# Square sums of q and k as two f32r products a tile later, in a stick-breaking attention trunk

## What is computed

```python
def odd_mixer(h, w_qkv, q_norm_g, k_norm_g, w_out):
    q, k, v = jnp.split(h @ w_qkv, 3, axis=-1)
    q = rms_norm(q.reshape(bsz, s_len, SB_HEADS, SB_HEAD_DIM), q_norm_g)   # 8 heads of 128
    k = rms_norm(k.reshape(bsz, s_len, SB_HEADS, SB_HEAD_DIM), k_norm_g)
    ...
# stick_breaking, for each block of queries:
    z = jnp.einsum('bhqd,bhkd->bhqk', qb, kb).astype(jnp.float32) * scale
    log_keep = jnp.where(mask, jax.nn.log_sigmoid(-z), 0.0)
    acc = lax.cumsum(log_keep, axis=3, reverse=True) - log_keep
    w = jnp.where(mask, jnp.exp(jax.nn.log_sigmoid(z) + acc), 0.0)
    outs.append(jnp.einsum('bhqk,bhkd->bhqd', w.astype(vb.dtype), vb))
```

## Time and profile before

| what | value |
|---|---|
| median of 3 runs | 2447.64 us (2446.96 to 2449.67) |
| the profiled execution | 2449.88 us, its span 2448.1 us |
| TensorE busy | 2408.2 us, 98% of the span |
| VectorE, ScalarE, GpSimd busy | 1583.0, 830.4, 595.5 us |
| mean granted clock of TensorE | 0.996 |
| TensorE's waits for others in 1180 to 1700 us | 6.6 us in all, 1.9 us the largest group |

### The profile page before, as it was taken

One profiled execution on the slowest core, in us unless ns is written; L12 is line 12 of the kernel. 1 busy time (PEld: TensorE's weight loads), 2 busy tenths in 40 slices (PEclk: granted clock), 3 DMA queues, 4 the chain that ended last, 5 costly groups with the idle time before them and its releaser, 6 DMA issues.

```text
span 2448.1 us, 31399 instructions
## 1 busy us (share of the span) xinstructions
PE 2408.2 (98%) x10938; PEld 1987.2 (81%) x10938; DVE 1583.0 (65%) x2543; ACT 830.4 (34%) x1489; POOL 595.5 (24%) x964
## 2 busy tenths in 40 slices
PE   6999999999999999999999999998999999999999
PEld 5888888888888888888778888887888888888887
DVE  6636777388667665765777777776587666665222
ACT  4102333144333340000466666664253333320001
POOL 4344333300000004455143333334100000015340
PEclk9999999999999999999999999999999999999999
DMA  8543446623342349666211111116323333456331
GB/s 284 173 138 99 134 133 205 204 78 112 104 129 95 112 129 351 225 228 210 78 53 44 44 43 44 43 54 222 121 74 108 121 104 111 129 202 229 147 121 69
DMA packets 268606, 324.40 MB, mean 133 GB/s; under 512 B 8458, under 2 KB 168356, under 8 KB 268324
## 3 DMA queue, kind: packets, MB, share of 16 engines
q1 hardware_dynamic: 239552, 257.45, 31.9%
q10 hardware_dynamic: 28900, 65.04, 7.5%
HBM read 240.67 MB, written 81.79 MB: 132 GB/s over the span
## 4 chain that ended last, share of the span: by engine, by line
PE 91%; DVE 3%; DMA 2%; issue 2%; POOL 1%; ACT 1%; SPq 0%; DVEq 0%; ACTq 0%; POOLq 0%
PE psG L911 24%; PE psG L917 23%; PE psG L916 23%; PE psZ L917 4%; PE psZ L916 4%; PE psZ L911 4%; PE psM L1347 1%; PE psO L911 1%; PE psG L1388 1%; PE psO L916 1%; PE psO L917 1%; PE psZ L1377 1%; DMA ada_raw<-in_ada_w 1%; DMA w_raw<-in_ev_w_in 1%; PE psM L962 1%
## 5 line engine op out<-in xcount | busy, mean ns | idle before, releaser
L883 POOL TENSOR_SCALAR w_split<-w_raw 128x256 fp32r<-128x256 f32 x448 | 199.4, 471 | 1773.3 <-DMA w_raw<-in_ffn_w_down 1091.6
L911 PE MATMUL psG<-h_hi,w_split 128*128 128x512 f32 x1080 | 436.1, 404 | 7.2 <-DVE h_lo L2168 3.8
L916 PE MATMUL psG<-h_lo,w_split 128*128 128x512 f32 x1080 | 425.4, 394 | 0.0
L917 PE MATMUL psG<-h_hi,w_split 128*128 128x512 f32 x1080 | 425.3, 394 | 0.0
L887 POOL TENSOR_TENSOR w_split<-w_raw,w_split 128x256 fp32r<-128x256 f32 x448 | 359.2, 832 | 0.0
L2714 DVE SCALAR_TENSOR_TENSOR xT<-psG,mod,xT 128x512 f32<-128x512 f32 x192 | 143.0, 749 | 212.3 <-PE psG L917 211.9
L911 PE MATMUL psG<-hid,w_split 128*128 128x512 f32 x704 | 276.3, 393 | 0.0
L911 PE MATMUL psG<-h_hi,f_w 128*128 128x512 f32 x704 | 275.2, 391 | 0.6 <-PE psG L917 0.6
L917 PE MATMUL psG<-hid,w_split 128*128 128x512 f32 x704 | 274.5, 390 | 0.0
L916 PE MATMUL psG<-hid,w_split 128*128 128x512 f32 x704 | 274.3, 390 | 0.0
L916 PE MATMUL psG<-h_lo,f_w 128*128 128x512 f32 x704 | 274.3, 390 | 0.0
(11 more groups left out here) (300 smaller groups left out, 4027.7 us busy)
## 6 DMA issues: line engine op xcount, KB each, us to landing
hid<-f_spill SPq DMA_DIRECT2D x44, 1024.0 KB, 9.4
f_spill<-f_stg SPq DMA_DIRECT2D x80, 512.0 KB, 2.7
f_raw<-in_ffn_w_gate SPq DMA_DIRECT2D x44, 512.0 KB, 3.9
f_raw<-in_ffn_w_up SPq DMA_DIRECT2D x44, 512.0 KB, 4.6
w_raw<-in_ffn_w_down SPq DMA_DIRECT2D x44, 512.0 KB, 6.1
ada_raw<-in_ada_w SPq DMA_DIRECT2D x40, 512.0 KB, 4.1
ada_raw<-in_ada_w ACTq DMA_DIRECT2D x40, 512.0 KB, 4.5
w_raw<-in_ev_w_in SPq DMA_DIRECT2D x28, 512.0 KB, 4.0
```

The costliest lines, as they stand in the source:

```text
L883: nc.gpsimd.tensor_scalar(slot[:, 0, part], raw[:, part], 1.0, 1.0, ALU.mult, ALU.mult).then_inc(hi_done, 1)
L911: mm = nc.tensor.matmul(o, st[0], mv[0], start=first, stop=False, **kw)
L916: nc.tensor.matmul(o, st[0], mv[1], start=False, stop=False, **kw)
L917: return nc.tensor.matmul(o, st[1], mv[0], start=False, stop=end, **kw)
```

## The change

Three edits. First, the square sums of q and k: ScalarE squares the copy twice, once to float32 and once to f32r (`s_sqh`), VectorE subtracts the two (`square_low`, behind the softplus of the slot) to `s_sql`, and TensorE makes two f32r products with the matrix of -1 in place of the float32 product; the factor -1/128 goes into ScalarE's Ln. The statistic and what follows it (`qkv_misc`, `qkv_second`, `qkv_dve`) go from slots 2, 4, 6, 8 to slots 3, 5, 7, 9 (`SUMMED`); v's steps stay. Copy and squares stay in slots 2, 4, 6, 8. Second, in `out1` GpSimd's slab 4 waits for the weights of all tiles but the last, and slab 5 for the last. Third, in `first_conv` slab 2's first four blocks go ahead of `first_direct`.

```diff
--- before.py
+++ after.py
@@ -110,6 +110,7 @@
 
 TAKEN = [2, 4, 6, 8, 10, NT]
 DONE = {t: e for e, t in enumerate(TAKEN)}
+SUMMED = {t + (e < 4): e for t, e in DONE.items()}
 ZRING = 3
 SRING = 3
 
@@ -280,7 +281,10 @@
         s_raw = [at("s_raw", WO + 32 * KB, [H]), at("s_raw1", WO + 8 * KB, [H])]
         s_sq = [at("s_sq", WO + 34 * KB, [H]), at("s_sq1", WO + 10 * KB, [H])]
         s_r = [at("s_r", WO + 36 * KB, [H]), at("s_r1", WO + 12 * KB, [H])]
-        s_t = at("s_t", WO + 38 * KB, [H])
+        s_t_off = (WO + 38 * KB, WO + 14 * KB)
+        s_t = [at(f"s_t{n}", s_t_off[n], [H]) for n in range(2)]
+        s_sqh = [at(f"s_sqh{n}", s_t_off[n], [H], F32R) for n in range(2)]
+        s_sql = [at(f"s_sql{n}", (WO + 34 * KB, WO + 10 * KB)[n], [H], F32R) for n in range(2)]
         s_vsb = at("s_vsb", WO + 40 * KB, [H])
         s_osb = at("s_osb", WO + 42 * KB, [2, H])
 
@@ -410,6 +414,8 @@
         fh_in = [sem(f"fh_in{n}") for n in range(4)]
         s_raw_cp = sem("s_raw_cp")
         s_rs = sem("s_rs")
+        s_sqh_in = sem("s_sqh_in")
+        s_sql_in = sem("s_sql_in")
         s_qk3 = sem("s_qk3")
         s_vhi = sem("s_vhi")
         s_zd = sem("s_zd")
@@ -871,6 +877,8 @@
                         if phase == "out1" and s == 4:
                             pool.wait_ge(s_qk3, 12 * SB_HEADS)
                         if phase == "out1" and s == 4:
+                            pool.wait_ge(s_wst, 3 + 2 * (NT * SB_HEADS - 1))
+                        if phase == "out1" and s == 5:
                             pool.wait_ge(s_wst, 3 + 2 * NT * SB_HEADS)
 
                         if phase == "out1" and s == 3:
@@ -1035,9 +1043,9 @@
                 x_turn(6)
                 k_major(0, (1,), (2, 3))
                 x_turn(7)
+                k_major(0, (2,), range(4))
                 pe.wait_ge(misc_read, M("norm0", 0, 1) - 1)
                 first_direct()
-                k_major(0, (2,), range(4))
                 first_cols(1, 0)
                 first_cols(1, 1)
                 x_root_pe(1)
@@ -1342,9 +1350,11 @@
                 hd = head[0] + i * head[1]
                 s, h, n = qkv_step(phase, e)
                 if s < 2:
-                    pe.wait_ge(s_raw_cp, 4 * hd + (n + 1))
-                    sq = s_sq[qk_pair(phase, n)]
-                    misc(phase, i, 2 * off + e, [lambda: nc.tensor.matmul(psM[:], ones_head, sq[:], start=True, stop=True)])
+                    pe.wait_ge(s_sql_in, 4 * hd + (n + 1))
+                    pair = qk_pair(phase, n)
+                    misc(phase, i, 2 * off + e, [
+                        lambda: nc.tensor.matmul(psM[:], split_c[:, 2], s_sqh[pair][:], start=True, stop=False),
+                        lambda: nc.tensor.matmul(psM[:], split_c[:, 2], s_sql[pair][:], start=False, stop=True)])
                 else:
                     bank_wait(pe, phase, i, 2 * off + e)
                     misc(phase, i, 2 * off + e, [lambda j=j: nc.tensor.transpose(psM[:, P * j:P * j + P], s_vsb[:, P * j:P * j + P], ident)
@@ -1426,8 +1436,8 @@
                         qkv_piece(phase, i, off, sum(PIECES[:t]) + n)
 
                 def stat(t):
-                    if t in DONE:
-                        qkv_misc(phase, i, off, DONE[t], hd_next)
+                    if t in SUMMED:
+                        qkv_misc(phase, i, off, SUMMED[t], hd_next)
 
                 for t in range(1, NT):
                     slot(hd, par, t, True, lambda: fill(t), lambda: stat(t))
@@ -1944,6 +1954,7 @@
                     fn(raw[:], psG[:, bank(phase, s)], ACT.Copy).then_inc(bank_read[bank(phase, s)], 1)
                     bank_wait(act, phase, i, s)
                     fn(sq[:], raw[:], ACT.Square).then_inc(s_raw_cp, 1)
+                    fn(s_sqh[pair][:], raw[:], ACT.Square).then_inc(s_sqh_in, 1)
                 else:
 
                     if phase != "qkv0":
@@ -1958,7 +1969,7 @@
                 m, h, n = qkv_step(phase, e)
                 if m < 2:
                     root = s_r[qk_pair(phase, n)]
-                    fn(root[:], psM[:], ACT.Ln, bias=EPS).then_inc(misc_read, 1)
+                    fn(root[:], psM[:], ACT.Ln, scale=-1.0 / HEAD, bias=EPS).then_inc(misc_read, 1)
                     act.wait_ge(misc_read, M(phase, i, 2 * off + e))
                     fn(root[:], root[:], ACT.Exp, scale=-0.5).then_inc(s_rs, 1)
                 else:
@@ -2021,8 +2032,8 @@
                         qkv_first(phase, i, off, DONE[t], hd_next)
 
                 def second_step(t):
-                    if t in DONE:
-                        qkv_second(phase, i, off, DONE[t], 1 - par, hd_next)
+                    if t in SUMMED:
+                        qkv_second(phase, i, off, SUMMED[t], 1 - par, hd_next)
 
                 for t in range(1, NT):
                     slot(hd, t, True, lambda: first_step(t), lambda: second_step(t))
@@ -2778,13 +2789,21 @@
                     dve.wait_ge(s_qk3, n0)
                     gain = qg[:, 0:1] if m == 0 else vecB[:, B_K:B_K + 1]
                     pair = qk_pair(phase, n)
-                    V.scalar_tensor_tensor(s_t[:], s_raw[pair][:], gain, s_r[pair][:], ALU.mult, ALU.mult).then_inc(s_qk3, 1)
+                    V.scalar_tensor_tensor(s_t[pair][:], s_raw[pair][:], gain, s_r[pair][:], ALU.mult, ALU.mult).then_inc(s_qk3, 1)
                     dve.wait_ge(s_qk3, n0 + 1)
-                    split([q[:, half(h)] for q in s_qk[par][m]], s_t[:], s_qk3, n0 + 2, s_qk3)
+                    split([q[:, half(h)] for q in s_qk[par][m]], s_t[pair][:], s_qk3, n0 + 2, s_qk3)
                 else:
                     dve.wait_ge(s_vhi, hd * 2 + (h + 1))
                     vv = slice(4 * h, 4 * h + 4)
                     V.tensor_tensor(s_v[par][1][:, vv], psM[:].rearrange("p (j c) -> p j c", c=P), s_v[par][0][:, vv].bitcast(F32), ALU.subtract).then_inc(misc_read, 1)
+
+            def square_low(phase, i, off, e, head):
+
+                hd = head[0] + i * head[1]
+                m, h, n = qkv_step(phase, e)
+                pair = qk_pair(phase, n)
+                dve.wait_ge(s_sqh_in, hd * 4 + (n + 1))
+                V.tensor_tensor(s_sql[pair][:], s_sq[pair][:], s_sqh[pair][:].bitcast(F32), ALU.subtract).then_inc(s_sql_in, 1)
 
             def softplus(hd, t):
 
@@ -2834,8 +2853,10 @@
             def head(phase, i, off, hd, hd_next, par):
 
                 def step(t):
-                    if t in DONE:
-                        qkv_dve(phase, i, off, DONE[t], 1 - par, hd_next)
+                    if t in SUMMED:
+                        qkv_dve(phase, i, off, SUMMED[t], 1 - par, hd_next)
+                    if t in DONE and DONE[t] < 4:
+                        square_low(phase, i, off, DONE[t], hd_next)
 
                 for t in range(1, NT):
                     slot(hd, t, True, lambda: step(t))
@@ -2845,12 +2866,20 @@
 
                 qkv_dve("qkv0", 0, 0, e, 0, (0, 0))
 
+            def first_low(e):
+
+                square_low("qkv0", 0, 0, e, (0, 0))
+
             for k in range(KT):
                 norm2.h_tile(1, k)
+                if k in (2, 3):
+                    first_low(k - 2)
                 if k == 5:
                     first_step(0)
             first_step(1)
             first_step(2)
+            first_low(3)
+            first_low(4)
             dve.wait_ge(x_out, 32)
             softplus(0, 0)
             first_step(3)
```

## The result

The changed kernel takes 2524.46 us (median, 2521.3 to 2527.11), against 2448.65 us for the kernel before: 1.0312 times as long, with a 95% interval of 1.03 to 1.0325. That is 75.8 us more, where 57.9 were forecast and 2518 us was the upper end of the range. The direction, the place and the two kinds of wait were right, the size was not.

What follows compares the result with a forecast made beforehand. TensorE, busy 59.91 of 60 us, was taken as the bound, with the round over three engines slower after the change. +46.9 + 10.5 + 0 + 1.0 - 0.5 = +57.9 us gave 2505.5 us from 2447.6; 8-in-10 range 2460 to 2518.

Steps and rivals of the forecast that it cites:

- The saving: On TensorE, each of 32 q and k statistics gets 0.43 us shorter, 13.8 us in all.
- The round over three engines: In each head, one q or k tile's end to the next takes 11.9 us against TensorE's 10.5: +6.7 us a head, +46.9.
- The direct chain: Last q or k tile to slot 10: 3.96 us needed, 1.58 available, so TensorE waits 2.4 us even with ScalarE and VectorE free.
- the rival at 2453 to 2464 us: Only the 2.4 us wait before slot 10 remains, 7 x 0.7 = +5 us plus clock 0 to 10.5; chance 0.13.
- The waits in one head: TensorE waits 2.9 us at tile e = 2's statistic, 1.4 at e = 3's, 4.0 at the next head's scores.
- The stretch by GpSimd: GpSimd's bursts slow VectorE on the round; left out of the sum, as a rival 0.8 us a head, 2511 us, chance 0.15.
- The clock: After the 4 us wait at each of seven heads' scores, a lower granted clock loses 1.5 us: +10.5 us, between 0 and that.
- The sum of both: Longer rounds and slower clock over seven heads: +46.9 and +10.5 us, 8.2 us a head.
- first projection: The first head's own projection: statistics save at most 1.7 us, low parts may lose 1.4; taken as 0.
- last +1.0: Last projection: earlier split of slab 4 makes slab 6's load meet the reload of x; +1.0 us, between 0 and +2.
- start -0.5: Kernel start: slab 2's products now wait for its split; from 0.75 us lost to 1.7 won, taken as -0.5.
- a 0.03: Case of a time over 2518 us, the clock staying low after each of the three waits; chance 0.03.

Runs made afterwards that it cites:

- The mended kernel: Changed square sums plus second copy buffer, scores waiting for nine steps, low part before softplus, without the slab 4 and `first_direct` edits: 2435.87 us, 0.9949 of before.
- short bursts: Changed kernel with GpSimd splitting only 4 of each 256 columns of the heads' q, k and v slabs: 2510.63 us, 1.0258 times before.
- Edit 2: Changed kernel with a second buffer for the copy of q and k (`s_raw` and `s_vsb` in turn): 2489.59 us, 1.0171 times before.
- Runs 4: GpSimd's splits in the heads cut to 4 of 256 columns, in the changed kernel (2510.63 us) and in the kernel before (2446.49 us).
- the move alone: Kernel before with the float32 statistic and its followers a tile later, nothing added: 2506.26 us; with GpSimd's splits cut to 4 of 256 columns, 2482.86 us.
- the control: Kernel before with GpSimd splitting only 4 of each 256 columns of the heads' q, k and v slabs: 2446.49 us, 0.9992 times before.
- run 6: Changed kernel with VectorE's low part of the squares ahead of the slot's softplus: 2519.05 us, 1.0286 times before.

## Why the prediction was right or wrong

- **The saving**, 0.43 us a statistic: right. The mended kernel shows it whole, 1.68 us a head and 12.5 us in all.
- **The round over three engines**: right in kind and, without GpSimd, in size: with short bursts the first statistic and the scores are 38.9 us apart, and the steps gave 39.0. The kinds of rows named for it came (the copy held by VectorE, the two kinds of waits, their lines). Edit 2 removes it and wins 34.9 us.
- **The direct chain** as a bound (3.96 us, wait of 2.4): its floor was wrong. It counted VectorE as free, but the low part itself holds VectorE just before, with 5.4 us of fixed work between it and the end of k. The measured distance is 5.43 us and the wait 3.6, also where the round is gone (run 2). In the sum it did no harm, since the long way round was taken there (the step from 6.3 us to 11.9 counts exactly this work); in the rival at 2453 to 2464 us it did, and a range drawn to 2460 leaned on it.
- **The waits in one head**: forecast 2.9, 1.4 and 4.0, together 8.3 us; measured 1.6, 2.1, 0.2 and 3.55 in the head shown, 7.8 on average. The first, at the statistic of e = 1, was not forecast. That the sum nearly fits is luck: the stretch lengthened the waits, and the slow clock took part of them, since work at a lower clock fills time that would have been a wait (0.2 us at the fourth statistic of the head shown, 2.0 in the heads where the clock stays whole up to it).
- **The stretch by GpSimd**: the step that failed. The prediction wrote "I leave it out of the sum", and its rival had 0.8 us a head, 5.6 us in all. Runs 4 give 11.2 to 13.8 us, 1.6 to 2.0 a head; in the move alone it is 21 to 23 us. The reason for 0.8, one burst on the round and two operations of it, was too small: q's three operations alone lose 1.07 us to the first burst, k's lose 0.64 to the next, and a low part takes 0.88 for 0.69. It also took one burst on the round, where the rows show two, one at q's first tile and one at k's. The row was the right one to read, and had to be counted for each operation under a burst.
- **The clock**: 1.5 us for the long wait was near. In five heads 1.6 to 1.7 us are lost behind the scores, in two 2.8, where the clock had fallen ahead of the scores and stayed low; those two heads take 29.8 us from the scores to the next statistic, the others 28.8 to 28.9, against 28.7 by the forecast (59.46 + 8.2 - 39.0). That is the smaller part of the miss, some 3 us. That a slower clock hides inside the round was right: with short bursts the way from the first statistic to the scores is 38.9 us in six heads, three of which lose 1.7 us to the clock in it and three nothing.
- **The sum of both**: forecast 8.2 us a head, measured 10.1 (9.5 in the first). 1.9 x 6 + 1.3 = 12.7 us. Most of it is the stretch: the short bursts give back 11.0 us of the span (13.8 by the medians, 11.2 less the control), and the clock behind the scores has the rest. Another 4.4 us of the miss are the distance between profiled executions and medians, which the range should have held.
- **The small terms** (first projection 0, last +1.0, start -0.5): their sum was +0.5, and the span outside the heads grew by 1.1 us. Alone, neither edit showed a difference in the time.
- **The range**: its upper end added the stretch and the clock as alternatives (2511, 2518). The stretch came together with the clock's 10.5 of the sum. The measured time lies where the prediction had only a 0.03, and not by that case's reason: the clock did not fall after each of the waits, and inside the round it cost nothing.

## What to carry to other kernels

When a step moves to a later slot in hand-ordered streams, walk the whole round from the release of the single buffer back to its next release, over every engine it visits, and compare it with the pace of the engine that sets the end: rounds of 11.5 to 12.6 us against 9.3 to 10.3 turned a saving of 12.5 us into a loss of 76, and the move alone made 58 of it. An engine with 15 us of idle time in 60 is not free at the moment at which it is asked. And once a round is as long as the pace, price each of its operations beside whatever runs on GpSimd, not at its usual duration.

## What the runs showed of the hardware

GpSimd's split of a slab lengthens VectorE's operations of 512 float32 columns by 0.1 to 0.5 us, most often by 0.4: the subtraction 1.11 us for 0.69, the gain and factor 0.88 to 1.22 for 0.75, the cast 0.85 for 0.43. The cast has one input only. The Trainium skill's page "GPSIMD Engine Reference", section "Specifications", says that GpSimd's interfaces are shared with VectorE's instructions that have two SBUF inputs or run in a 2-port mode. The subtraction agrees with the first half of that sentence; the cast's doubling would fit the second, but no trace here shows the mode in which it ran. In the kernel before this is hidden by slack (2.6 us for the bursts of all heads, not to be told from none), on the closed round it costs 11 to 23 us.

How long a wait was does not by itself say what the granted clock does behind it. At the same place in the first head a wait of 1.78 us left it at 1.00 in the changed kernel, and one of 1.80 us was followed by 0.74 and 0.84 over 4 us each in run 6; in the changed kernel it stayed at 1.00 after 2.11 us and fell after 1.99. Behind the waits of 2.7 to 3.6 us at the scores it was low in every head. And what a fall costs depends on who sets the end: 1.7 us lost inside the round lengthened nothing, 1.6 to 2.8 us lost behind the scores came nearly whole. So the sum of the waits and the lost clock do not simply add; each must be read beside the round of the engine that is the slowest.
